# The order of long and short matmuls in feature-major sums over weight slots

## The reference

```
proj = h @ w_in[i]                    # gates: three blocks of 1024 columns of it
u = causal_depthwise_conv(h @ w_up[i], conv_w[i], conv_b[i])
q, k, v, g = jnp.split(x @ w_in, ...)              # retention
return jnp.square(jax.nn.relu(x @ w1)) @ w2        # MLP of the second half
```

## Time and profile before

| | |
|---|---|
| runs, median (lowest to highest) | 2067.94 us (2067.27 to 2068.09) |
| profiled execution, span from its first to its last instruction | 2067.1 us |
| profiled execution's own time | not given apart from the three runs; the median is 0.8 us above the span |
| TensorE busy | 2047.0 us, 99% |
| VectorE, ScalarE, GpSimd busy | 1540.0, 1054.1, 170.6 us |
| read from memory | 374.87 MB |

### The profile page before, as it was taken

One profiled execution on the slowest core, in us unless ns is written; L12 is line 12 of the kernel. 1 busy time (PEld: TensorE's weight loads), 2 busy tenths in 40 slices (PEclk: granted clock), 3 DMA queues, 4 the chain that ended last, 5 costly groups with the idle time before them and its releaser, 6 DMA issues.

```text
span 2067.1 us, 26974 instructions
## 1 busy us (share of the span) xinstructions
PE 2047.0 (99%) x11155; PEld 1755.9 (85%) x11155; DVE 1540.0 (75%) x1704; ACT 1054.1 (51%) x1236; POOL 170.6 (8%) x94
## 2 busy tenths in 40 slices
PE   8999999999999999999999999999999999999998
PEld 6988888898988888778888988888888888788887
DVE  6888899789978767666766787666876667567665
ACT  5574655456565545455433665344654345455432
POOL 2001121020112105000000000000000005000000
PEclk9999999999999999999999999999999999999999
DMA  8544555564455556555665555655366556455653
GB/s 279 173 139 167 185 193 190 181 195 143 143 194 194 184 184 193 169 183 183 206 197 180 177 186 184 220 183 149 142 202 206 192 183 210 143 186 181 212 196 102
DMA packets 244739, 377.67 MB, mean 183 GB/s; under 512 B 14101, under 2 KB 179210, under 8 KB 244618
## 3 DMA queue, kind: packets, MB, share of 16 engines
q1 hardware_dynamic: 244474, 375.42, 55.2%
q10 hardware_dynamic: 144, 0.52, 0.1%
HBM read 374.87 MB, written 1.05 MB: 182 GB/s over the span
## 4 chain that ended last, share of the span: by engine, by line
PE 92%; DVE 4%; DVEq 1%; ACT 1%; DMA 0%; issue 0%; SPq 0%
PE bank L738 46%; PE acc L738 44%; PE bank L736 2%; DVE slot_lo L2043 2%; DVEq L2038 1%; ACT slot_hi L1510 1%; PE acc L736 0%; DMA slot<-in_w_in 0%; DVE arena L2798 0%; DVE arena L2300 0%; DVEq L2302 0%; DVE arena L2804 0%; DVE arena L2132 0%; ACT arena L1505 0%; DVE arena L2419 0%
## 5 line engine op out<-in xcount | busy, mean ns | idle before, releaser
L2043 DVE TENSOR_TENSOR slot_lo<-slot,slot_hi 128x2048 fp32r<-128x2048 f32 (+1 forms) x343 | 787.9, 2304 | 271.0 <-ACT slot_hi L1510 270.1
L1510 ACT ACTIVATE slot_hi<-slot 128x2048 fp32r<-128x2048 f32 (+1 forms) x343 | 650.4, 1904 | 379.2 <-DMA slot<-in_mlp_w 310.1
L738 PE MATMUL acc<-slot_hi,split 128*128 128x512 f32 x2236 | 713.2, 392 | 4.8 <-DVE slot_lo L2043 3.1
L738 PE MATMUL bank<-split,slot_hi 128*128 128x512 f32 (+1 forms) x2292 | 536.2, 366 | 0.3 <-ACT arena L1505 0.3
L738 PEld LDWEIGHTS acc<-slot_hi,split 128*128 128x128 f32 x2236 | 420.9, 188 | 93.8 <-issue 5.7
L738 PEld LDWEIGHTS bank<-split,slot_hi 128*128 128x128 f32 x2292 | 403.7, 189 | 62.0 <-issue 1.5
L738 PE MATMUL acc<-slot_lo,split 128*128 128x512 f32 x1118 | 436.7, 391 | 0.0
L738 PE MATMUL bank<-split,slot_lo 128*128 128x256 f32 x2022 | 320.7, 282 | 0.0
L738 PEld LDWEIGHTS bank<-split,slot_lo 128*128 128x128 f32 x2022 | 290.8, 191 | 17.1
L738 PEld LDWEIGHTS acc<-slot_lo,split 128*128 128x128 f32 x1118 | 210.7, 188 | 41.0 <-issue 1.0
L738 PE MATMUL bank<-slot_hi,split 128*128 128x512 f32 (+1 forms) x804 | 218.4, 380 | 1.2 <-ACT split L1527 0.9
(11 more groups left out here) (249 smaller groups left out, 1541.0 us busy)
## 6 DMA issues: line engine op xcount, KB each, us to landing
slot<-in_mlp_w SPq DMA_DIRECT2D x128, 1024.0 KB, 5.4
slot<-in_ret_w_in SPq DMA_DIRECT2D x48, 1024.0 KB, 5.2
slot<-in_w_up SPq DMA_DIRECT2D x40, 1024.0 KB, 5.1
slot<-in_w_in SPq DMA_DIRECT2D x37, 1024.0 KB, 5.3
slot<-in_w_down SPq DMA_DIRECT2D x22, 1024.0 KB, 4.9
slot<-in_ret_w_o SPq DMA_DIRECT2D x16, 1024.0 KB, 4.9
slot<-in_lru_w_in SPq DMA_DIRECT2D x10, 1024.0 KB, 5.4
slot<-in_w_out SPq DMA_DIRECT2D x8, 1024.0 KB, 4.9
```

The costliest lines, as they stand in the source:

```text
L738: i = nc.tensor.matmul(o, w, m, start=start, stop=stop)
L1510: A(whi[u.r][:, 0:u.cols], raw[u.r][:, 0:u.cols], ACT.Copy).then_inc(slot_hi[u.r], 1)
L2043: TTO(wlo[u.r][:, 0:u.cols], raw[u.r][:, 0:u.cols], f32(whi[u.r][:, 0:u.cols]), ALU.subtract)\
```

## The change

The second loop over `k` goes away, and its matmul moves into the first: long and short alternate, k-tile by k-tile. The same 16 matmuls with the same operands go into the same bank; the first and the last of them are the same as before.

```diff
                     for k in range(DT):
                         mm(o[:, :].rearrange("p (i s) -> p i s", i=2), w[0][:, k, j * P:(j + 1) * P], hTs[:, :, k, :],
                            k == 0, False)
-                    for k in range(DT):
                         mm(o[:, 0:S], w[1][:, k, j * P:(j + 1) * P], hT[0][:, k, :], False, k == DT - 1,
                            end if k == DT - 1 else None)
                     if between and j == 0:
                         between()
```

## The result

The changed kernel takes 2076.57 us, median of five runs (2075.05 to 2076.78), against 2068.09 (2067.27 to 2068.97) for the kernel before on the same chip: 1.0036 times as long, 95% interval 1.0025 to 1.0047 from the runs' ratios. A later set of five gave 2076.47 against 2067.98, 1.0041 (1.0027 to 1.0055). It is slower by some 8 us.

What follows compares the result with a forecast made beforehand. PE, busy 99% of the span, was taken to bound the kernel. 1984 pairs x 0.0023 us, less 5 us of round trips, gave -0.4 us: 2067.94 to 2067.5 us, range 2049.5 to 2082.

Steps and rivals of the forecast that it cites:

- PE bounds, everything passes through: Whole kernel: PE is busy 99% of the span, so any gain or loss in matmul pace reaches the end in full.
- No wait is added, banks and buffers do not matter: In the sums of `two_sums`: no matmul newly waits for weights, banks are released as before; only each matmul's neighbour changes.
- The price of a pair, p = 0.349: One long and its short alternating in the sums: 0.349 us against 0.3467 linear, over 1984 pairs; chance 35% for 0.348 to 0.350.
- the long's term, 0.232: Each 512-column matmul in the alternation costs 0.232 us, the average of five longs behind shorts, against 0.2267 steady.
- The short's term, 0.115 to 0.117: Each 256-column matmul in the alternation costs 0.115 to 0.117 us, as the first two behind a long, against 0.120 steady.
- The -5 us of round trips that go away: All 248 sums: each sum's long-to-short-to-long switch has a surcharge of 0.02 us, 5 us in all, that goes away.
- The longs never find their steady pace: In the alternating sums: longs need five in a row to recover, so each costs 0.232 us instead of 0.227.
- even pace: Rival for the sums: alternation runs at the linear 0.3467 us a pair, only the 5 us goes: 2063 us; chance 15%.
- switches cost: Rival for the sums: a long behind a short is late, its weight load having only 120 ns; 2073 to 2081 us, 20%.
- The objection that a pair has no second pitch: Argument against dearer pairs in the sums: the 0.24 us pitch is the second behind eight shorts, which a pair lacks.
- A round trip costs 0.02 us and the surcharge does not grow with the shorts: At length switches, long to short to long: 0.02 us over the linear price, the same behind 8 or 144 shorts.
- The early start of the short is borrowed: First short behind a long: its pitch of 0.11 us against 0.12 is given back by the longs that follow, 0.03 late.

Runs made afterwards that it cites:

- the first two experiments: Against the changed kernel: short matmuls take the high part of the weights (span 2073.9 us); short matmuls go into the other sum's bank (span 2075.8 us).
- the runs with 384 columns: Each short matmul streams 384 columns instead of 256: alternating as in the changed kernel, span 2182.5 us; eight and eight as in the kernel before, 2181.7 us.
- by fours: Against the changed kernel: four long, then four short matmuls, twice in a sum; span 2071.3 us.
- by twos: Against the changed kernel: two long, then two short matmuls, four times in a sum; 2067.29 us against 2067.98 for the kernel before, 0.9994.
- Sixteen and sixteen: Against the kernel before: both banks of a slot opened, 8 + 8 long, then 8 + 8 short matmuls; 2066.69 us against 2069.13, 0.9988.

## Why the prediction was right or wrong

- *PE bounds, everything passes through.* Right: the long waits, the chain and the other engines did not move; 7.1 us in the sums and 0.5 in the products behind them make 7.6 of the span's 7.7.
- *No wait is added, banks and buffers do not matter.* Right, and shown by the first two experiments.
- *The price of a pair, p = 0.349.* This step failed, and in it the long's term, 0.232. On the slow beat the longs take 241, 236 and 233 ns, mean 0.2367. The short's term, 0.115 to 0.117, was right: 113, 117 and 120 ns average 0.1167. With 210 sums at 0.3533 and 38 at 0.3467 the settled price is 0.3523, and 1984 x (0.3523 - 0.349) is 6.6 of the 7.5 us between the forecast (-0.4) and the sums (+7.1). What was wrong behind the number is the assumption that a pair is a mix of what single switches show. Behind a single switch the longs take 233, 236, 228, 233 and 231 ns; a pitch of 241 is not among them. Nor would another choice have saved it: the first long and the first short behind a switch, 233 + 113, give 0.346, less than the linear price.
- *The -5 us of round trips that go away.* Too large by 2 us. Over the linear price the kernel before paid 3.3 us in the 166 sums behind a sum, and saved 0.4 in the 69 behind a product: 3 us in the sums. The other 1.7 us were paid by the products behind the sums, and they stayed. Against that, sums behind a product still start cheaply after the change (227 + 113 ns for the first pair), and all sums together stay some 1.1 us under the settled price, so that 0.9 is left.
- *"The longs never find their steady pace."* Right for 210 sums. For the other 38 the price is the linear one, as the rival "even pace" had it, though even there a long takes 230 ns and not its steady 227. One kernel shows both prices, which the prediction had not foreseen.
- *The rival "switches cost"* had the outcome, 2073 to 2081, and p (0.352 to 0.356). That is in part luck: it put the long too low (0.234 to 0.236) and the short too high (0.118 to 0.120), and its reason, too little cover for the weight load, is refuted by the runs with 384 columns. The objection that a pair has no second pitch did not hold: the slow beat's 241 ns is above any pitch of the single switches.
- *A round trip costs 0.02 us and the surcharge does not grow with the shorts.* Right as a reading, wrong as a law: by fours and by twos it is 0.017 and 0.003 a round trip.
- *The early start of the short is borrowed.* It held: no alternation of 512 and 256 columns has settled below 0.346. Two small slips changed nothing: 0.351 lies 4.3 ns over the linear price, not 4.6, and 2067.94 is 0.8 above the span, not 0.9.
- By the Trainium skill's rule on loads pulled ahead (TensorE: Matmul & The Clock Gate, "Step-by-step: what each phase is for") the order would be free. The trace of the changed kernel disagrees by 20 ns in three pairs.

What makes the beats is open. The runs exclude the weight buffers, the banks, the load's cover and the clock. Equal lengths have no surcharge, the surcharge of 512 and 256 comes in steps of 20 ns in three pairs, and a few nanoseconds in the first pitch go with one beat or another. That fits a matter of phase inside PE, but no run here looks further in, and this is not shown.

## What to carry to other kernels

Where PE is the bound and its matmuls have two lengths, do not alternate them singly without measuring: here that lost 0.4%. Sixteen and sixteen won 0.1% over eight and eight, twos were level with eights, and fours were dearer, so a finer order is not always worse. Count pitches between starts, not busy times. Do not price an alternation from single switches: neither the mean of the recovery (0.349) nor the first pitches behind a switch (0.346) gave the 0.353 that it settled on. A settled alternation can have a beat of its own that no single switch shows, and only running it tells.

## What the runs showed of the hardware

- Matmuls with a weight load each take 226.7 ns for 512 columns and 120.0 for 256 in steady runs, so 13.3 ns and 0.417 ns for a column; with 384 columns the last two of eight take the 173 ns that follow from it.
- Behind a single switch from 256 to 512 columns the first five longs take 233, 236, 228, 233 and 231 ns; behind one from 512 to 256 the first two shorts take 113 and 119.
- 512 and 256 columns in alternation settle at one of two prices, 346.7 or 353.3 ns a pair, and keep it over whole sums; 512 and 384 settle at 406.7 or 413, against a linear 400.
- For a sum behind another sum the order by twos takes 2.787 us, eights 2.793, fours 2.807, and single alternation 2.830 on the slow beat and 2.773 on the even one.
- Behind the same wait of 2.6 us PE has a stretch at the 1.2 GHz level in the trace of the kernel before (0.94 over 30 us) and none in the trace by twos (1.00). It is worth some 1.5 us, as much as several of the effects studied here.
